# Expert outputs added onto the gated residual in token rows

## The reference, cut to what matters

```
def layer_stream(x, mod, ...):
    ...
    x = x + gate1[:, None] * out
    h = modulate(rmsnorm(x, p['norm_ffn']), shift2, scale2)
    x = x + gate2[:, None] * ec_moe(h, p['w_router'], p['b_router'], p['w_e1'], p['w_e3'], p['w_e2'])
    return x, C, n, m, s
def ec_moe(h, ...):
    aff = softmax(h @ w_router + b_router);  topv, topi = top_k(aff per expert, cap)
    xe = h[topi]
    ye = ((silu(xe @ w1) * (xe @ w3)) @ w2) * topv
    return zeros.at[topi].add(ye)
```

## Time and profile before

| | |
|---|---|
| three runs, median | 1885.4 us (1881.7 to 1889.7) |
| profiled execution | 1894.1 us, its span 1892.3 us |
| PE busy | 1708.9 us (90%) |
| DVE, ACT, POOL busy | 580.4, 368.3, 103.8 us |
| DMA share of 16 engines in slices 24 to 37 | 9 tenths or more, 391 to 412 GB/s |
| routing block | about 1007.6 to 1038 us |
| expert block | about 1038 to 1851 us |
| residual block | about 1851 to 1892.3 us |

### The profile page before, as it was taken

One profiled execution on the slowest core, in us unless ns is written; L12 is line 12 of the kernel. 1 busy time (PEld: TensorE's weight loads), 2 busy tenths in 40 slices (PEclk: granted clock), 3 DMA queues, 4 the chain that ended last, 5 costly groups with the idle time before them and its releaser, 6 DMA issues. The chain is left out here.

```text
span 1892.3 us, 33654 instructions
## 1 busy us (share of the span) xinstructions
PE 1708.9 (90%) x15258; PEld 971.0 (51%) x15258; DVE 580.4 (31%) x1325; ACT 368.3 (19%) x759; POOL 103.8 (5%) x101
## 2 busy tenths in 40 slices
PE   4799998999899898878983899999999999999963
PEld 2366665546455464668971344444444444444442
DVE  4469981012113131357546001111111111111124
ACT  3343332121211213145423100000000000000001
POOL 2600000000000000000001000000000000000000
PEclk8799998999899899989996899999999999999986
DMA  9335455000202021043305799999999999999903
GB/s 397 127 104 178 163 185 193 27 29 1 100 11 101 11 78 45 21 180 122 134 34 223 294 366 398 404 399 404 404 401 402 402 401 406 401 402 412 391 8 118
DMA packets 57204, 420.08 MB, mean 222 GB/s; under 512 B 10964, under 2 KB 17620, under 8 KB 27236
## 3 DMA queue, kind: packets, MB, share of 16 engines
q1 hardware_dynamic: 49476, 386.45, 51.4%
q0 software_dynamic: 7584, 31.47, 5.4%
HBM read 391.34 MB, written 24.42 MB: 220 GB/s over the span
## 5 line engine op out<-in xcount | busy, mean ns | idle before, releaser
L1694 PE MATMUL bank<-place,x 128*32 128x384 f32 x3120 | 258.2, 489 | 0.9 <-ACT x L1757 0.9
L1694 PE MATMUL bank<-ring_tail,x 128*32 128x384 f32 x3024 | 249.8, 488 | 1.4 <-issue 1.4
L1694 PEld LDWEIGHTS bank<-place,x 128*32 128x32 f32 x3120 | 100.5, 110 | 147.4 <-issue 143.9
L1694 PEld LDWEIGHTS bank<-ring_tail,x 128*32 128x32 f32 x3024 | 98.3, 110 | 145.1 <-issue 143.8
L1788 DVE TENSOR_SCALAR hT<-bank,gvr 32x256 f32<-32x256 f32 (+1 forms) x192 | 92.1, 480 | 249.6 <-PE bank L1724 247.0
L1799 DVE TENSOR_TENSOR hid<-sq,bank 128x384 f32<-128x384 f32 x48 | 23.7, 550 | 439.8 <-issue 362.3
L1095 PE MATMUL bank<-place,hT 128*128 128x512 f32 x320 | 138.0, 592 | 0.0
L1724 PE MATMUL bank<-ring_tail,hidT 128*32 128x256 f32 x2304 | 130.0, 384 | 6.1 <-issue 6.1
L239 PE MATMUL bank<-hT,xT 128*128 128x512 f32 x256 | 133.7, 604 | 1.1 <-ACT qk L249 0.9
L1724 PE MATMUL bank<-place,hidT 128*32 128x256 f32 x2304 | 128.0, 379 | 0.0
L1438 PE MATMUL bank<-a_h,w_h 128*128 128x320 f32 x320 | 102.4, 320 | 19.7 <-DVE w_l L1510 17.1
(11 more groups left out here) (357 smaller groups left out, 1935.5 us busy)
## 6 DMA issues: line engine op xcount, KB each, us to landing
place<-w_e_dram SPq DMA_DIRECT2D x97, 1536.0 KB, 11.4
ring_tail<-w_e_dram SPq DMA_DIRECT2D x95, 1536.0 KB, 11.3
place<-w_ada_dram SPq DMA_DIRECT2D x12, 2048.0 KB, 9.2
xT<-w_gate_dram POOLq DMA_DIRECT2D x8, 1024.0 KB, 6.3
place<-w_qk_dram SPq DMA_DIRECT2D x4, 2048.0 KB, 9.0
place<-w_vo_dram SPq DMA_DIRECT2D x4, 2048.0 KB, 10.7
place<-w_pAB_dram SPq DMA_DIRECT2D x4, 1536.0 KB, 6.8
hT<-gates_dram SPq DMA_DIRECT2D x4, 1280.0 KB, 6.3
```

What stands on the lines that cost most here:

```text
L1694: mm = pe.matmul(PS[bank + j][TJ * g:TJ * g + TJ, 0:FC], x[:, e % 2, 2 * c + k, TJ * j:TJ * j + TJ], w[:, k, FC * g:FC * g + FC], start=(c ...
```

## The change

The array `moe_dram` is not cleared any more: it starts as the residual itself, in token rows. In the routing block TensorE transposes `xT` too, ScalarE copies the rows into one of two buffers `xrow` and stores each tile from its own queue (the only DMAs that ScalarE issues in this kernel). `gate2` is spread by small matmuls into bank 0, so that each of its four groups of 32 partitions holds one 256-channel quarter for latent and for context tokens; VectorE multiplies expert outputs with it in `take_y`. `xT` is free after the transposes, and holds `nfin` (the gain of the last norm, copied over all partitions by the host) and `gate2`. `down(15)` writes banks 3 and 4 and does not wait for `y_ready`. In the last block each token tile is loaded, squared and summed along its row, scaled, multiplied with the gain and stored by itself; the output is now in token rows. Semaphores were renamed and shared (`piece_in`, `u_in` and the wait for the loads into `part_in`; the steps of the routing block into `route_step` and `route_turned`), which alters no order.

```diff
-                pool.wait_ge(sem("zero_set"), 1)
-                for t in range(NT):
-                    pool.dma_start(ar["moe"][t * P:(t + 1) * P, :], zero[:]).then_inc(sem("moe_zero"), 16)
-                pool.wait_ge(sem("moe_zero"), 16 * NT)
...
+        def parts_before(s):
+            return 16 * L if s < NQ else 0
+
+        def pieces_of(s):
+            return (len(moe_pieces) - s + NR - 1) // NR
...
+        xflat = xT[:].rearrange("p k t -> p (k t)")
+        nfin = xflat[:, 0:D]
+        gate2 = xflat[:, D:D + 512].rearrange("p (s d) -> p s d", s=2)
         with ExitStack() as st:
+            xrow = sb("xrow", [P, 2, D], F32, st)
+            spread = sb("spread", [P, KD, 2, TJ], F32, st)
...
+                sp.wait_ge(sem("x2_turned"), NT)
+                sp.dma_start(nfin, ar["nfin"]).then_inc(sem("nfin_in"), 16)
...
+                pe.wait_ge(sem("gate2_spread"), 1)
+                for g in range(NG):
+                    for s in range(2):
+                        for b in range(2):
+                            o = 256 * s + P * b
+                            mm = pe.matmul(PS[0][TJ * g:TJ * g + TJ, o:o + P], spread[:, 2 * g + b, s, :], ident,
+                                           start=True, stop=True)
+                mm.then_inc(sem("route_turned"), 1)
+                for t in range(NT):
+                    pe.wait_ge(sem("htok_ready"), NT)
+                    if t >= 2:
+                        pe.wait_ge(sem("xrow_ready"), t - 1)
+                    for k in range(KD):
+                        mm = pe.transpose(PS[1 + 2 * (t % 2) + k // 4][:, (k % 4) * P:(k % 4 + 1) * P],
+                                          xT[:, k, t * P:(t + 1) * P], ident)
+                    mm.then_inc(sem("x2_turned"), 1)
+                pe.wait_ge(sem("route_step"), 4)
...
+                act.activation(spread[:], bc(modT[:, 40:48, :].unsqueeze(3), [P, KD, 2, TJ]), ACT.Copy
+                               ).then_inc(sem("gate2_spread"), 1)
+                for t in range(NT):
+                    act.wait_ge(sem("x2_turned"), t + 1)
+                    if t >= 2:
+                        act.wait_ge(sem(f"xrow_out{t % 2}"), 16 * (t // 2))
+                    for x in range(2):
+                        ins = act.activation(xrow[:, t % 2, x * 512:(x + 1) * 512], PS[1 + 2 * (t % 2) + x][:, :],
+                                             ACT.Copy)
+                    ins.then_inc(sem("xrow_ready"), 1)
+                    act.wait_ge(sem("xrow_ready"), t + 1)
+                    act.dma_start(ar["moe"][t * P:(t + 1) * P, :], xrow[:, t % 2, :]).then_inc(sem(f"xrow_out{t % 2}"), 16)
+                act.wait_ge(sem("route_turned"), 3)
+                act.activation(gate2.rearrange("p s d -> p (s d)"), PS[0][:, :], ACT.Copy
+                               ).then_inc(sem("gate2_ready"), 1)
+                for x in range(2):
+                    act.wait_ge(sem(f"xrow_out{x}"), 16 * ((NT + 1 - x) // 2))
...
+            def y_bank(e):
+                return 6 if e + 1 < E else 3
...
-                    if e:
+                    if e and e + 1 < E:
...
-                                    mm = pe.matmul(PS[6 + j // 2][TJ * g:TJ * g + TJ, 256 * (j % 2):256 * (j % 2) + 256],
+                                    mm = pe.matmul(PS[y_bank(e) + j // 2][TJ * g:TJ * g + TJ, 256 * (j % 2):256 * (j % 2) + 256],
...
-                            ins = dve.tensor_scalar(ys[TJ * j:TJ * j + n, e % 2, 256 * g:256 * g + 256],
-                                                    PS[6 + j // 2][TJ * g:TJ * g + n, 256 * (j % 2):256 * (j % 2) + 256],
-                                                    gvr[TJ * g:TJ * g + n, j, e:e + 1], None, ALU.mult)
+                            ins = dve.scalar_tensor_tensor(
+                                ys[TJ * j:TJ * j + n, e % 2, 256 * g:256 * g + 256],
+                                PS[y_bank(e) + j // 2][TJ * g:TJ * g + n, 256 * (j % 2):256 * (j % 2) + 256],
+                                gvr[TJ * g:TJ * g + n, j, e:e + 1], gate2[TJ * g:TJ * g + n, j // 2, :],
+                                ALU.mult, ALU.mult)
                     ins.then_inc(sem("y_ready"), 1)
 
+                dve.wait_ge(sem("gate2_ready"), 1)
...
+            y = sb("y", [P, NT, D], F32, st)
+            junk = sb("junk9", [P, D], F32, st)
+            ss = sb("ss", [P, NT], F32, st)
+            rs = sb("rs", [P, NT], F32, st)
             block = st.enter_context(nc.Block())
 
             @block.sync
             def _(sp):
                 for t in range(NT):
+                    sp.dma_start(mt[:, t, :], ar["moe"][t * P:(t + 1) * P, :]).then_inc(sem(f"part_in{t}"), 16)
+                for t in range(NT):
+                    sp.wait_ge(sem("y_done"), t + 1)
+                    sp.dma_start(out["y"][t * P:(t + 1) * P, :], y[:, t, :]).then_inc(sem("out_done"), 16)
+                sp.wait_ge(sem("out_done"), 16 * NT)
 
             @block.scalar
             def _(act):
+                def root(t):
+                    act.wait_ge(sem("ms_inverse"), t + 1)
+                    act.activation(rs[:, t:t + 1], ss[:, t:t + 1], ACT.Sqrt).then_inc(sem("rms_row"), 1)
+
+                for t in range(NT):
+                    act.wait_ge(sem(f"part_in{t}"), parts_before(t) + 16 * pieces_of(t) + 16)
+                    if t:
+                        act.wait_ge(sem("row_square"), t)
+                    act.activation(junk[:], mt[:, t, :], ACT.Square, accum_out=ss[:, t:t + 1]
+                                   ).then_inc(sem("row_square"), 1)
+                    if t:
+                        root(t - 1)
+                root(NT - 1)
 
             @block.vector
             def _(dve):
                 v = chain(dve, "dve")
+
+                def finish(t):
+                    dve.wait_ge(sem("rms_row"), t + 1)
+                    dve.scalar_tensor_tensor(y[:, t, :], mt[:, t, :], rs[:, t:t + 1], nfin, ALU.mult,
+                                             ALU.mult).then_inc(sem("y_done"), 1)
+
+                dve.wait_ge(sem("nfin_in"), 16)
+                for t in range(NT):
+                    dve.wait_ge(sem("row_square"), t + 1)
+                    v(dve.tensor_scalar(ss[:, t:t + 1], ss[:, t:t + 1], 1.0 / D, EPS, ALU.mult, ALU.add))
+                    dve.reciprocal(ss[:, t:t + 1], ss[:, t:t + 1]).then_inc(sem("ms_inverse"), 1)
+                    if t:
+                        finish(t - 1)
+                finish(NT - 1)
```

More of the change, by code:

```diff
@@ L354, in _ @@
                 pool.memset(meanw[:], 1.0 / D).then_inc(sem("meanw_set"), 1)
-                pool.memset(zero[:], 0.0).then_inc(sem("zero_set"), 1)
                 p = chain(pool, "pool")
                 pool.wait_ge(sem("s5bc_in"), 16)
-                pool.wait_ge(sem("b_factor"), 1)
+                pool.wait_ge(sem("s5_step"), 3)
                 wr = bc(t5[:, 7, :].unsqueeze(2), [P, GN, GC])
@@ L419, in _ @@
                 v(dve.tensor_tensor(t5[:, 6, :], aim, t5[:, 0, :], ALU.mult))
-                dve.tensor_tensor(t5[:, 1, :], are, t5[:, 0, :], ALU.mult).then_inc(sem("s5_z"), 1)
+                dve.tensor_tensor(t5[:, 1, :], are, t5[:, 0, :], ALU.mult).then_inc(sem("s5_step"), 1)
                 MAGIC = 1.5 * 2.0 ** 23
@@ L1361, in ring @@
             return ring_tail[0][:, s - len(SLOTS), :]
+        def parts_before(s):
+            return 16 * L if s < NQ else 0
+        def pieces_of(s):
+            return (len(moe_pieces) - s + NR - 1) // NR
         def load_piece(sp, n):
             name, e, c = moe_pieces[n]
-            sp.dma_start(ring(n), ar["w_e" + name[1]][e, c]).then_inc(sem(f"piece_in{n % NR}"), 16)
+            sp.dma_start(ring(n), ar["w_e" + name[1]][e, c]).then_inc(sem(f"part_in{n % NR}"), 16)
         with ExitStack() as st:
@@ L1619, in _ @@
                 dve.tensor_scalar(topf[:, CAPL:CAP], topf[:, CAPL:CAP], float(LAT), None,
-                                  ALU.add).then_inc(sem("top_ready"), 1)
-                dve.wait_ge(sem("top_turned"), 1)
+                                  ALU.add).then_inc(sem("route_step"), 1)
+                dve.wait_ge(sem("route_turned"), 4)
                 dve.tensor_copy(gvr[:].rearrange("p j e -> p (j e)"), PS[7][:, 0:NJ * E])
@@ L1815, in _ @@
                 for t in range(NT):
[L1816 to L1819, removed]
-                sp.wait_ge(sem("yT_out"), 16 * KD)
-            @block.tensor
-            def _(pe):
-                pe.wait_ge(sem("mt_in"), 16 * NT)
-                for k in range(KD):
-                    if k >= 3:
-                        pe.wait_ge(sem("x3_ready"), k - 2)
-                    for t in range(NT):
-                        dst = PS[k % 3][:, t * P:(t + 1) * P] if t < 4 else PS[3 + k % 3][:, 0:CTX]
-                        mm = pe.transpose(dst, mt[:, t, k * P:(k + 1) * P], ident)
-                    mm.then_inc(sem("moe_turned"), 1)
-                pe_mean_square(pe, 2)
```

(21 more changed lines are left out.)

53 lines of the change are left out of this document (25 added, 28 removed).

## The result

The changed kernel takes 1860.8 us (median of four runs, 1856.6 to 1870.0) against 1884.8 us (1881.7 to 1889.7) of the kernel before on the same chip: ratio 0.9852, with 95% interval 0.9815 to 0.9889 (the quotient of the two medians is 0.9872). The profiled execution took 1856.6 us, its span is 1854.7 us.

What follows compares the result with a forecast made beforehand. TensorE was taken to bound the expert loop, with the DMA queue some 28 us in hand. Terms -8.1 + 0.3 - 22.9 + 3.0 = -27.7 us gave 1857.7 us against the median of 1885.4; range 1848 to 1873.

Steps and rivals of the forecast that it cites:

- Handover, -8.1 us: Last expert: `down(15)` no longer waits for `y_ready`; 6.08 us of pause and 2.07 us of slow clock go.
- surcharge of 0.3 for the new form: Last expert's twelve VectorE instructions as `scalar_tensor_tensor`: +0.3 us, bounds 0 and +0.7.
- Rival (c): Handover: something other than bank 6 holds `down(15)`, the 8.1 us stay, 1866 us; chance 0.05.
- Cover of `take_y`: Expert loop: about 1.6 us in hand before `turn_x`; up to 0.62 us per new-form instruction costs nothing.
- Rival (d): Expert loop: new form costs 0.75 us, TensorE waits at `turn_x`, 50 us lost in all, 1908 us; chance 0.03.
- Last block, -22.9 us: Final block: each token tile handled by itself, ending at 1869.4 in place of 1892.3; bounds -25 and -15.
- Rival (b): Final block gives less, as Square/Sqrt table switches would add 10 us, some 2 hidden; 1866 us; chance 0.08.
- Routing block, +3.0 us: Routing block: residual row stores end it 2.5 us later, plus 0.5 at the first gather; bounds 0 and +18.
- the three waits: Routing block, row stores 0, 2, 4: landing at 1028, about 1033 and 1040, the last sharing engines for six us.
- The 0.5 us for the gather: First gather: a megabyte beside it is 2.6 us of traffic, of which 0.5 us was taken.
- Rival (a): Routing block: row stores land late, costing 15 us in place of 3, 1870 us; chance 0.12.
- Start, 0 us: First block: the five zero stores go, but lie beside ScalarE's modulate chain, which ends the block; 0 us.

Runs made afterwards that it cites:

- five-buffer version: Changed kernel with five row buffers in hT in place of two, so no copy waits for a store; ratio 0.9817 to the kernel before.
- version with late pieces: Changed kernel with pieces 8 and 9 and the gain loaded after the first gathers; ratio to the kernel before 0.9819 with two row buffers, 0.9818 with five.

## Why the prediction was right, and where it was not

**The total.** Forecast -27.7 us; in the trace behind `gidx` -25.2 us, in the medians -24.1 us. All terms that moved had the right sign, and 1860.8 us lies in the range. The sum came out nearer than its largest error: the routing block cost 4.2 us more than forecast, while the last block gave 1.0 us more and the handover, with the new form, 0.6 us more. (The best ends of the terms add to -33.2 and not -33.4 us, which changes nothing.)

**Handover, -8.1 us.** Measured -8.4 with `take_y(15)`, where -7.8 were forecast with the surcharge of 0.3 for the new form. The surcharge is nil: the new form costs the 0.48 us that the straight line gave. That the pause made the clock fall, and so cost 2 us beyond itself, is shown by putting it back. Rival (c) is out.

**Cover of `take_y`.** 1.6 us in hand were read from two rows of one expert. Three more instructions (1.6 us) cost nothing in the loop, eight (4.3 us) made TensorE wait 2.45 us per expert, so some 1.9 us were in hand. Rival (d) had its place right and its point of decision nearly; its price had 2.07 us too much per expert, since the clock did not fall in pauses of 2.45 us as it did in one of 6.1.

**Last block, -22.9 us.** Measured -23.9. The order was as worked out (table load behind the second Square, five results of VectorE in a row, last store 2.7 us where 3.0 were taken). This block was not changed by itself in any experiment but for the table; its term is read from the two traces. Rival (b) is out: one table load.

**Routing block, +3.0 us: the term that was mis-sized.** It cost 7.2 us (6.1 to 7.7 us over the seven profiles with this block unaltered). For a 512 KB store an estimate from the Trainium skill ("DMA: Bandwidth & Descriptors", section Anatomy of one DMA — SWDGE (gpsimd) path; 2.0 us and the bytes at 436 GB/s, a fit to DMAs issued by GpSimd) is 3.2 us; store 2 with 3.6 us comes near it, stores 0 and 4 do not. Of the three waits two were right: store 0 was given 7.2 us and took 7.3, store 2 was given 3.6 and took 3.6. That they agree to 0.1 us is luck, since store 0 was placed by judgement between bounds of 2.3 and 10.7 us. The step that failed is "its store shares the engines with pieces 8 and 9: six us"; it took 10.4 us, about as long as the quickest h2 store of the earlier trace rows; the engines were at their full share from 1024 to 1029. The sum stayed near its lower bound because two of the three waits would fall "where the engines are partly free"; it was the third that set the block's end, 7.2 us late instead of 2.5. The 0.5 us for the gather were 0 in this version, only because the block ended so late that the traffic was over; in the five-buffer version they became 4.2 us. Rival (a) named this mechanism with 15 us; half of that came.

**Start, 0 us.** Right for the first block itself, as the stores put back show. The prediction had no term for the rest of the front, and the 12.4 us there can't be booked: a part is the spread of single executions (3.5 us between two of the same program), and a part of up to some 6 us may follow from the stores' removal through the clock in the mixer, which the profiles suggest and the timed runs neither show nor exclude.

## What to carry over

Here the extra traffic cost time where a wait stood beside large transfers already issued; store 0 met full engines too (7.3 us), and as the version with late pieces shows, that alone delayed nothing that mattered. So ask for each short store or gather that somebody waits for what was issued just before it, and move what is needed late (here two pieces used some 30 us later) behind it. A removed pause of TensorE is worth its own length and, if it was long enough for the clock to fall, the slow matmuls behind it. Where the program's start varies by 10 us from run to run, compare the parts of the trace between fixed points before believing a difference of spans; but before calling such a difference chance, sort all profiles by whether they have the edit.

## What the runs showed of the hardware

TensorE's granted clock fell after a pause of 6.1 us (0.84 from 1820 to 1830, just behind it; 144 matmuls in 10.0 us instead of 7.96), and did not fall in pauses of 2.45 us every 50 us (1.00). In the mixer the same hundred us ran at 0.90, 0.93 or 0.97 in different executions, at both of the last two also with the very same program. A 512 KB store took 2.6 us with little beside it (store 4 with late pieces), 3.6 us just after the traffic had gone, 7.3 to 10.4 us beside others; the same gather of 80 rows took 4.0 us or 8.3 us.
